# Retention scores and values as three rounded products, with the scores ahead of the gate's units

## What is computed

```python
proj = h @ w_in
q, k, v, g = jnp.split(proj, [RET_QK, 2 * RET_QK, 2 * RET_QK + RET_V], axis=-1)
q = rotary(q, pos); k = rotary(k, pos) * (RET_DK ** -0.5)
o = retention_chunkwise(q, k, v)          # per head: (q k^T * decay) v, causal
oc = o - mean(o); o = oc * rsqrt(mean(oc * oc) + EPS)
return (silu(g) * o) @ w_out
```

## Time and profile before

| | us |
|---|---|
| median of 3 runs | 2823.46 |
| the 3 runs | 2819.07, 2823.46, 2824.46 |
| the profiled execution | 2819.14 |
| its span in the profile | 2817.3 |
| PE busy in the span | 2790.8 (99%) |
| DVE, ACT, POOL busy | 1790.2, 1100.7, 444.0 |

### The profile page before, as it was taken

How to read it: one execution, slowest core, us unless ns; L and a number is a source line. 1 busy time by engine, 2 the same in 40 slices (tenths; PEclk the granted TensorE clock), 3 DMA queues, 4 the chain that set the end, 5 groups by cost and what they waited for, 6 DMA issues and landing times.

```text
span 2817.3 us, 38185 instructions
## 1 busy us (share of the span) xinstructions
PE 2790.8 (99%) x15294; PEld 2336.1 (83%) x15294; DVE 1790.2 (64%) x2551; ACT 1100.7 (39%) x1559; POOL 444.0 (16%) x391
## 2 busy tenths in 40 slices
PE   8999999999999999999999999999999999999999
PEld 5778778788888888888888888889998887888887
DVE  6456456777667567777646797675775538554443
ACT  4233235333332443323445433234554448442322
POOL 0101111686562100000211100001002124100000
PEclk9999999999999999999999999999999999999999
DMA  7433232455648555454313465553553431132222
GB/s 313 145 136 131 101 120 99 144 190 194 218 158 275 185 172 179 158 189 157 120 68 131 151 202 191 203 172 127 180 180 120 163 116 36 61 105 97 98 97 83
DMA packets 124241, 420.12 MB, mean 149 GB/s; under 512 B 21920, under 2 KB 22432, under 8 KB 122400
## 3 DMA queue, kind: packets, MB, share of 16 engines
q1 hardware_dynamic: 102544, 373.15, 38.4%
q0 software_dynamic: 9520, 35.53, 3.8%
q10 hardware_dynamic: 12000, 9.01, 1.0%
HBM read 400.39 MB, written 19.86 MB: 149 GB/s over the span
## 4 chain that ended last, share of the span: by engine, by line
PE 94%; DVE 3%; ACT 1%; issue 1%; DMA 1%; POOL 0%; SPq 0%; ACTq 0%; DVEq 0%; POOLq 0%
PE bk L112 87%; PE turns L112 6%; PE turns L115 2%; DVE wl L121 1%; ACT wh L118 1%; DVE O L121 0%; DVE sp L121 0%; DMA X<-in_x_dram 0%; ACT tm L118 0%; DMA Ux<-U_d 0%; DVE tm L133 0%; DMA U_d<-tm 0%; ACT L118 0%; POOL pr L121 0%; DVE ctm L133 0%
## 5 line engine op out<-in xcount | busy, mean ns | idle before, releaser
L121 DVE TENSOR_TENSOR wl<-raw,wh 128x1024 fp32r<-128x1024 f32 x506 | 658.2, 1302 | 424.5 <-ACT wh L118 406.1
L112 PE MATMUL bk<-HH,wh 128*128 128x512 f32 x2048 | 802.6, 392 | 3.7 <-DVE wl L121 2.9
L112 PE MATMUL bk<-HH,wl 128*128 128x512 f32 x2048 | 798.0, 390 | 0.0
L112 PE MATMUL bk<-HL,wh 128*128 128x512 f32 x2048 | 787.4, 389 | 0.0
L118 ACT ACTIVATE wh<-raw 128x1024 fp32r<-128x1024 f32 x506 | 531.5, 1052 | 432.4 <-PE bk L112 428.2
L112 PEld LDWEIGHTS bk<-HH,wh 128*128 128x128 f32 x2048 | 384.9, 188 | 89.6 <-issue 6.1
L112 PEld LDWEIGHTS bk<-HL,wh 128*128 128x128 f32 x2048 | 384.9, 188 | 80.5 <-issue 1.0
L112 PEld LDWEIGHTS bk<-HH,wl 128*128 128x128 f32 x2048 | 384.8, 188 | 79.7
L124 DVE CUSTOM_DVE_ANT_0 ttr<-ar,cB 128x1024 f32<-128x1024 f32 x240 | 307.8, 1283 | 7.5 <-DMA ar<-in_ada_dram 0.3
L112 PE MATMUL bk<-gh,wh 128*128 128x512 f32 x704 | 274.2, 389 | 0.0
L112 PE MATMUL bk<-gh,wl 128*128 128x512 f32 x704 | 273.9, 389 | 0.0
(11 more groups left out here) (407 smaller groups left out, 3871.2 us busy)
## 6 DMA issues: line engine op xcount, KB each, us to landing
raw<-in_wts_dram SPq DMA_DIRECT2D x506, 512.0 KB, 3.5
ar<-in_ada_dram SPq DMA_DIRECT2D x176, 512.0 KB, 3.9
first<-in_adaK_dram SPq DMA_DIRECT2D x8, 1024.0 KB, 20.1
F_d<-CA POOLq DMA_DIRECT2D x8, 512.0 KB, 5.2
E_d<-stg ACTq DMA_DIRECT2D x16, 256.0 KB, 2.5
M_d<-K_d POOLq DMA_DIRECT2D x8, 512.0 KB, 10.4
EB<-E_d POOLq DMA_DIRECT2D x8, 512.0 KB, 5.6
EB<-M_d POOLq DMA_DIRECT2D x8, 512.0 KB, 7.3
```

What stands on the lines that cost most here:

```text
L112: return Nothing() if self.e is None else self.e.matmul(*a, **k)
L121: return Nothing() if self.e is None else self.e.tensor_tensor(*a, **k)
```

## The change

Scores and values are no longer fp32 products. `qk`, v and the decayed scores are each split in two halves, as the weights are, and each product becomes three fp32r matmuls. ACT writes the high halves `qh`, `vh`, `Sh`, DVE the low halves `ql`, `vl`, `Sl`. The decayed scores go to `tm` and `pr` first, since their two halves are made from them. To fit, the halves share places with `sg`, `O`, `oh` and `ol`, and `attend` is cut in two: `scores(h)` stands ahead of the gate's units and `values(h)` behind. Head 3 has its scores behind the first gate unit and its values behind the second. The v banks are now given back by DVE (`vl`), not by ACT.

```diff
-        r.vv = at("vv", Z + 20480, [P, 4, L])
+        r.vh = at("vh", Z + 20480, [P, 4, L], R)
+        r.vl = at("vl", Z + 36864, [P, 4, L], R)
-        r.St = at("St", Z + 36864, [P, 4, L])
+        r.qh = at("qh", Z + 45056, [P, 4, L], R)
+        ql, ql3 = at("ql", Z + 28672, [P, 4, L], R), at("qlast", Z, [P, 4, L], R)
...
-                                  lambda k, tt: HL[:, k, tt * 128:tt * 128 + 128], xw, VB, lambda tt: (act, ("vv", h, tt))):
+                                  lambda k, tt: HL[:, k, tt * 128:tt * 128 + 128], xw, VB, lambda tt: (vec, ("vl", h, tt))):
...
-            def attend(h):
+            def scores(h):
+                e.wait_ge(*vec.of(("ql", h, 3)))
                 for mt in range(4):
                     b = 4 + mt % 2
                     n = L - 128 * mt
+                    keys, rows = slice(mt * 128, mt * 128 + 128), slice(mt * 128, L)
                     claim(e, b)
-                    e.wait_ge(*vec.of(("rot", h, 1)))
-                    e.matmul(BK[b][:, :n], r.qk[:, 2, mt * 128:mt * 128 + 128], r.qk[:, 0, mt * 128:L], start=True, stop=False)
-                    e.matmul(BK[b][:, :n], r.qk[:, 3, mt * 128:mt * 128 + 128], r.qk[:, 1, mt * 128:L],
-                             start=False, stop=True).then_inc(*pe.up(("s", h, mt)))
+                    for i in range(2):
+                        e.matmul(BK[b][:, :n], r.qh[:, 2 + i, keys], r.qh[:, i, rows], start=(i == 0), stop=False)
+                        e.matmul(BK[b][:, :n], r.qh[:, 2 + i, keys], r.ql[h][:, i, rows], start=False, stop=False)
+                        mm = e.matmul(BK[b][:, :n], r.ql[h][:, 2 + i, keys], r.qh[:, i, rows], start=False, stop=(i == 1))
+                    mm.then_inc(*pe.up(("s", h, mt)))
                     bank[b] = (vec, ("st", h, mt))
+
+            def values(h):
                 for j in range(4):
                     claim(e, GB[j])
-                    e.wait_ge(*act.of(("vv", h, 3)))
+                    e.wait_ge(*vec.of(("vl", h, 3)))
                     for mt in range(4):
-                        e.wait_ge(*vec.of(("st", h, mt)))
-                        mm = e.matmul(BK[GB[j]][:, mt * 128:L], r.vv[:, mt, j * 128:j * 128 + 128], r.St[:, mt, :L - 128 * mt],
-                                      start=(mt == 0), stop=(mt == 3))
+                        e.wait_ge(*vec.of(("sl", h, mt)))
+                        o, w = BK[GB[j]][:, mt * 128:L], slice(j * 128, j * 128 + 128)
+                        e.matmul(o, r.vh[:, mt, w], r.Sh[h][mt][:, :], start=(mt == 0), stop=False)
+                        e.matmul(o, r.vh[:, mt, w], r.Sl[h][mt][:, :], start=False, stop=False)
+                        mm = e.matmul(o, r.vl[:, mt, w], r.Sh[h][mt][:, :], start=False, stop=(mt == 3))
...
+            for h in (1, 2):
+                qkv(h, lambda: mean(h - 1), lambda: var(h - 1), lambda: turned(h - 1))
+                run(out(h - 1))
+                scores(h)
+                run(gate(h))
+                values(h)
             qkv(3, lambda: mean(2), lambda: var(2), lambda: turned(2))
-            attend(3)
             for m in gate(3):
+                if m == 0:
+                    scores(3)
                 if m == 1:
+                    values(3)
+                if m == 2:
                     mean(3)
...
+            def qk_low(h, i):
+                e.wait_ge(*act.of(("qh", h, i)))
+                e.tensor_tensor(r.ql[h][:, i, :], r.qk[:, i, :], r.qh[:, i, :].bitcast(F), ALU.subtract).then_inc(*vec.up(("ql", h, i)))
...
             def decayed(h):
                 for mt in range(4):
-                    e.tensor_tensor(r.St[:, mt, :n], BK[4 + mt % 2][:, :n], r.D[:, h, :n], ALU.mult).then_inc(*vec.up(("st", h, mt)))
+                    e.tensor_tensor((tm + pr)[mt][:, :n], BK[4 + mt % 2][:, :n], r.D[:, h, :n], ALU.mult).then_inc(*vec.up(("st", h, mt)))
+                    if mt:
+                        s_low(h, mt - 1)
+                s_low(h, 3)
...
             def gate(h):
                 for m in range(4):
                     lo(e, last_unit(("g", h), m, 8) + 2)
+                    if m == 0:
+                        decayed(h)
```

More of the change, by code:

```diff
@@ L941, in ret_pe @@
             qkv(0)
+            scores(0)
             run(gate(0))
[L943 to L951, removed]
+            values(0)
+            for h in (1, 2):
[4 more added lines that the diff above has]
+                values(h)
             qkv(3, lambda: mean(2), lambda: var(2), lambda: turned(2))
-            attend(3)
             for m in gate(3):
+                if m == 0:
+                    scores(3)
                 if m == 1:
+                    values(3)
+                if m == 2:
                     mean(3)
             for m in out(2):
-                if m == 0:
+                if m == 1:
                     var(3)
@@ L978, in vv @@
                     hi(e, base[("v", h)] + q + 2)
+                    if h == 0 and q == 2:
+                        for i in range(4):
+                            qk_high(0, i)
                 for tt in range(4):
@@ L982, in vv, with qk_high, s_high @@
                         e.wait_ge(*pe.of(("o", h - 1, 3)))
-                    e.activation(r.vv[:, tt, :], BK[VB[tt]][:, :], ACT.Copy).then_inc(*act.up(("vv", h, tt)))
+                    e.activation(r.vh[:, tt, :], BK[VB[tt]][:, :], ACT.Copy).then_inc(*act.up(("vh", h, tt)))
+            def qk_high(h, i):
+                e.wait_ge(*vec.of(("rot", h, i // 2)))
+                if h:
+                    e.wait_ge(*vec.of(("ol", h - 1, 3)))
+                e.activation(r.qh[:, i, :], r.qk[:, i, :], ACT.Copy).then_inc(*act.up(("qh", h, i)))
+            def s_high(h):
+                for mt in range(4):
+                    e.wait_ge(*vec.of(("st", h, mt)))
+                    if 0 < h < 3:
+                        e.wait_ge(*pe.of((("out", h - 1), 7)))
+                    e.activation(r.Sh[h][mt][:, :], (tm + pr)[mt][:, :L - 128 * mt], ACT.Copy).then_inc(*act.up(("sh", h, mt)))
             def gate(h, beside=lambda m: None):
@@ L1034, in ret_act @@
             vv(0)
-            gate(0)
+            gate(0, lambda m: s_high(0) if m == 0 else None)
             attend(0)
@@ L1046, in ret_act, with last_gate, last_out @@
                 if h < 2:
[L1047 to L1053, removed]
+                    out(h, lambda m: qk_high(h + 1, m) if m < 4 else None)
+                    gate(h + 1, lambda m: s_high(h + 1) if m == 0 else None)
+                    attend(h + 1)
+            for i in range(4):
+                qk_high(3, i)
+            def last_gate(m):
+                if m == 1:
+                    s_high(3)
+                if m == 2:
+                    attend(3)
+                if m == 3:
+                    squares(3)
+            gate(3, last_gate)
+            def last_out(m):
+                if m == 1:
+                    root(3)
+                if m >= 4:
+                    high(3, m - 4)
+            out(2, last_out)
             for m in range(8):
@@ L1125, in out @@
                     add_to(e, ("out", h), m, GB[m % 4], X, L, 0, 2)
+                    if h < 2 and m < 4:
+                        qk_low(h + 1, m)
             def project(h):
@@ L1141, in project @@
                     lo(e, base[("v", h)] + q + 2)
+                    if h == 0 and q == 2:
+                        for i in range(4):
+                            qk_low(0, i)
+                v_low(h)
             def gate(h):
@@ L1145, in gate @@
                     lo(e, last_unit(("g", h), m, 8) + 2)
+                    if m == 0:
+                        decayed(h)
             project(0)
             gate(0)
-            decayed(0)
             need_mod(e, 0, 2)
-            for h in range(1, 4):
+            for h in range(1, 3):
                 project(h)
[L1153 to L1156, removed]
+                out(h - 1)
+                gate(h)
+            project(3)
+            for i in range(4):
+                qk_low(3, i)
             for m in range(4):
                 lo(e, last_unit(("g", 3), m, 8) + 2)
-                if m == 2:
+                if m == 0:
+                    decayed(3)
+                if m == 3:
                     centred(3)
@@ L1163, in ret_vec @@
                 add_to(e, ("out", 2), m, GB[m % 4], X, L, 0, 2)
-                if m == 1:
+                if m == 2:
                     inverse(3)
```

35 lines of the change are left out of this document (24 added, 11 removed).

## The result

The changed kernel takes 2826.18 us (median of 20 runs, 2821.27 to 2830.16), the kernel before on the same chips 2819.46 (20 runs, 2817.27 to 2824.81). The ratio is 1.0020, with a 95% interval of 1.0014 to 1.0026: at the edge of what can be told from no change, and on the slower side. The ratio stands for 5.6 us; the two medians lie 6.7 apart. The forecast was 2828.0, or 1.0016 of the median that it started from.

A forecast was written before the change was run, and what follows sets the result against it. PE, busy 99% of the span, was taken to bound the kernel. Stream -6.2, waits +8.3 and clock +2.4 gave +4.5 us on the median 2823.46, so 2828.0 us, range 2820 to 2837.

The forecast's parts named there:

- PE's stream: Scores and values on PE: six sets of four blocks per head, 1.91 us each; 6.2 us less in all four heads.
- Rival 1: Scores and values: a rounded 128-column matmul costs 0.22 like fp32; +12.0 us, 2835.5; chance 0.16, including rounding failing at 384 and below.
- rival 2: Scores and values: 128 columns cost 0.067 (2824.5 us), or each rounded matmul a quarter of fp32 (2821.2 us); chance 0.13.
- The waits: PE waiting behind DVE at block 2 of heads 0 to 2, `qlast` and a bank in `out(1)`: 8.3 us more in sum.
- the bank in `out(1)`: Third row of `out(1)` wants bank 0 before DVE's third `vl` gives it back: PE waits 0.9 us.
- The old wait: PE's wait for `St` in head 3 of the kernel before goes: 0.8 us, 1.0 with the refilling of PE.
- the 0.1 at block 2 of head 3: Scores of head 3: PE waits 0.1 us more at block 2, since the unit's split stands between.
- The clock: PE falls to half clock behind the longer new waits, 1.6 us per fall; one to two falls taken, +2.4 us.
- The sum: Whole kernel: -6.2 of stream, +8.3 of waits, +2.4 of clock make +4.5 us.
- The base: Median of the kernel before, 2823.46 us, from which the forecast of 2828.0 started.
- the leaning: Whole kernel: no measurable change, leaning slower; forecast case 0.66, within 0.2% 0.62, slower by over 0.2% 0.33.

The follow-up runs named there:

- e1: Changed kernel with the decay of the scores ahead of the gate unit's split and `ttr` on DVE in heads 0 to 2: 2819.84 us, ratio 1.0002.
- e4: Kernel before with the new order alone (scores ahead of the gate, values behind), products still fp32, nothing split: 2823.34 us, ratio 1.0012.
- e6: Changed kernel with two extra multiplications on DVE ahead of the decay in heads 0 to 2: 2836.74 us, ratio 1.0055.
- e2: Changed kernel with head 3 alone reordered: ACT rounds q before v, DVE does `qlast`, decay, `vl`, then the split: 2823.97 us, ratio 1.0016.
- e8: Changed kernel in its own order, only the blocks of 128 columns as fp32 products: 2823.89 us, ratio 1.0013.
- e3: Changed kernel with the edits of e1 and e2, and `vl` reordered in heads 1 to 3: 2814.51 us, again 2814.47; ratios 0.9985 and 0.9980.
- e5: Kernel of e3 with 128-column blocks as fp32 products (scores of heads 0 to 2, all values): 2818.5 us, again 2814.75; ratios 0.9996 and 0.9982.
- e7: Kernel of e3 with only the scores' 128-column blocks in heads 0 to 2 as fp32 products: 2813.17 us, ratio 0.9974.

## Why the prediction was right, point by point

**PE's stream.** Forecast 1.91 us for a set, measured 1.92. The one price without a row, 0.116 for 128 columns, was 0.111 with all that follows it, so the 0.112 of the one-column matmuls held as a floor. Rival 1 (0.22) and the 0.067 of rival 2 are out. The Trainium skill (TensorE: Matmul & The Clock Gate, section Back-to-back issue gap) gives about 81 ns for 128 columns in a stream of loads and matmuls; for these rounded operands the trace has 111, and the measurement decides. By the Trainium skill's four passes for true fp32 (FP8 and Floating Point Precision, section TensorE Precision Notes), an estimate, three rounded passes would be three quarters of an fp32 product. At 512 columns that is nearly so (0.68 us against 0.86, from 99.33 to 102.34 with the 384 columns in proportion); at 128 it is wrong, 0.33 against 0.22.

**The waits.** Forecast and measured, in us: head 0 2.5 and 2.44; head 1 2.1 and 2.03; head 2 0.9 and 0.89; `qlast` in head 3 2.8 and 2.69; the bank in `out(1)` 0.9 and 0.84. The old wait went, and the 0.1 at block 2 of head 3 did not come. e1, e4 and e6 show that this is the cause: taken away, the time comes back; with fp32 the waits stay; made longer by 1.5, they are longer by 1.5.

**The clock.** Forecast one to two falls in retention, in the profile two, 3.2 us instead of 2.4. One was not where the lengths would put it: the wait of 2.44 in head 0 had none behind it, the shorter one of head 1 did. That this one execution has just these two is luck in part. Over all executions the changed kernel loses 6.1 us by its clock and the kernel before, beside the experiments, 3.1, so the 2.4 is right in size there too. These are the stretches behind the waits of heads 0, 1 and 3:

```profile
85.46:88.87 3.41, 3.41 (x20) 2.92 (x19) 2.04 (x6) 0.83 (x3) 0.00 (x0) 1.00 0.51 180
188.87:192.29 3.42, 3.42 (x11) 2.74 (x11) 1.64 (x6) 0.73 (x2) 0.00 (x0) 0.50 0.40 141
376.61:380.02 3.41, 3.06 (x8) 2.48 (x9) 1.52 (x3) 0.85 (x1) 0.00 (x0) 0.50 0.21 60
```

**The sum.** -6.0 of stream (24 x 1.92 = 46.1 against 4 x 13.01 = 52.0), +7.9 of waits (8.9 less the old 1.0), +3.2 of clock: +5.1, where the forecast had +4.5. The forecast left out the slower first matmul behind each new wait; it took it in for the old one only. In heads 0 to 2 and at the bank it is 0.11 each, 0.4 in all, so +5.5. The two profiles bear it out. PE leaves the same wait at 55.73 before and here:

```profile
57.79 0.47 PE L112 MATMUL turns<-wh,HH 128*128 128x512 f32 x1 [1.68 <-DVE wl L121]
```

and it starts on `Ux` at 857.43 in the kernel before and at 865.05 in the changed one:

```profile
857.43 2.08 PE L112 MATMUL turns<-Ux,EB 128*64 128x64 f32 x64 [1.74 <-DMA Ux<-U_d]
```

So 801.70 and 807.26 us lie between, 5.6 more. Of the 8.3 us between the spans 2.1 arise ahead of that, in the start of the program, which the change doesn't touch; there the changed kernel's profile has a fall of the clock that the other hasn't:

```profile
21.62:25.03 3.41, 3.12 (x10) 2.02 (x14) 1.62 (x4) 0.00 (x0) 0.00 (x0) 0.50 1.01 428
```

**What was off.** The base: the three runs gave a median of 2823.46, twenty gave 2819.46. The ratio of 1.0016 came out as 1.0020, while the 2828.0 was too high by 1.8, since two misses, 4.0 on the base and 2.2 on the difference of the medians, went against each other; that part is luck. And the leaning: I gave two chances in three to a case of +4.5 us, while the difference of the medians is 6.7, just over the 5.6 that I set as the bound. The terms of the sum, 5.5, agree with the 5.6 of the ratio; the 6.7 is within its interval too (3.9 to 7.3 us).

## What to carry to other kernels

When work is moved on the engine that bounds the kernel, write down for its every semaphore when it arrives and what stands ahead of the producer in the producer's queue, as it is after the move. Here a saving of 6 us was there, and the new waits cost 8.9, of which 5.4 were a split and a `ttr` ahead of a decay; two lines in another order give those back. For narrow operands, count matmuls and not columns: at 256 columns three rounded passes (0.36) still pay against one fp32 product (0.43, from 102.34 to 102.77 in the kernel before), and at 128 the fp32 product is cheaper (0.22 against 0.33). Judge a wait by the profile and not by a difference of medians of 2 us, which falls of the clock can hide, as in e2. And a gain of a few microseconds ahead of a load that sets its own time can come back as a longer wait.

## What the runs showed of the hardware

**The same idle time costs differently from execution to execution.** PE's wait of 2.44 in head 0 stands in three profiles with the same length. Behind it the clock stays at 1.00 (2.4 GHz) in the changed kernel and in e8, and falls to 0.50 (1.2 GHz) in e2. The wait of 2.03 in head 1 is followed by a fall in the changed kernel, and by none in e2 and e8. In e2, behind the first and the second:

```profile
85.90:89.30 3.40, 3.40 (x10) 2.65 (x9) 1.15 (x4) 0.63 (x2) 0.00 (x0) 0.50 0.24 94
188.90:192.30 3.40, 3.40 (x22) 3.04 (x23) 2.55 (x7) 1.58 (x4) 0.00 (x0) 1.00 0.70 253
```

The wait of 2.0 us at some 490 us, outside of what is changed, has a fall behind it in one of the two profiles of e3 and none in the other. The other waits in retention: 2.69 (in three profiles), 3.48, 3.96, 2.34 (e6) and 2.09 (e8) had a fall behind them, 1.85, 1.44 and 0.89 none. Outside of retention, a wait of 2.73 for `Ux` in e8 had none either. So between 2.0 and 2.7 us the length of a wait doesn't tell whether it costs only itself or 1.6 us more.

**The clock also falls with no wait ahead of it.** The 24 fp32 matmuls of one column behind the output rows of head 3 are in every profile. In eight of the twelve (e2, e4, e7, e8 and both of e3 and of e5) the clock falls 2.3 to 4.0 us after the first of them, for 3.41 us, in e2 for 6.83. In the other four (before, changed, e1, e6) it stays at 1.00. What tells the two groups apart is open.

**The price of a narrow matmul shows at its neighbours.** The successor of the first of the three rounded matmuls of 128 columns starts after 0.06, the next two take 0.11, and the 512 columns behind them take 0.28 instead of 0.227. Read alone, the first of these looks like half the price.

**A longer wait can cost more in clock than in time.** The 5.1 us for `Ux` in e5 come with 13.65 us at half clock, and these cost 5.9 us, more than the wait; behind the waits of 2 to 4 us that had a fall, it was 3.4 us at half clock and some 1.6 of cost.
